# Products that read activations and write sums from the last column on, with weight halves at 64 and 128 bytes

## The reference

```python
z = jnp.einsum("bsd,de->bse", rmsnorm(x, g_mix), w_in)        # and w_qb, w_kvb
x = x + einsum(sigmoid(ga) * (oa @ w_oa) + sigmoid(gb) * (ob @ w_ob), w_o)
x = x + einsum(relu(einsum(rmsnorm(x), w_up)) ** 2, w_down)
x = x + sigmoid(einsum(rmsnorm(x), w_ple_gate)) * einsum(p, w_ple)
# second block, two layers: a gated delta rule (gdn_w_in, gdn_w_out), then forgetting
# attention (w_kv, fox_w_q, fox_w_o), each followed by
f = (silu(gu[..., :2816]) * gu[..., 2816:]) @ w_out            # gu = h @ w_in
x = x + rms_norm(f, post_ffn_norm)
```

## Time and profile before

| | |
|---|---|
| median of three runs | 2165.18 us |
| profiled execution | 2162.32 us |
| its span, first to last instruction | 2160.5 us |
| mean granted TensorE clock | 0.987 of 2.4 GHz |
| TensorE matmuls | 2095.5 us busy, 10710 instructions |
| TensorE weight loads | 1697.5 us busy, 10710 |
| VectorE, ScalarE, GpSimd | 1146.3, 816.6, 38.4 us busy |

### The profile page before, as it was taken

The page is one execution under the profiler, slowest core; times in us unless marked ns, Lnnn a source line. Parts: engine busy times, 40 slices in busy tenths (PEclk is TensorE's granted clock), DMA queues, the critical chain, the costliest instruction groups (busy, mean ns, idle before and its releaser), DMA issues. The chain is left out here.

```text
span 2160.5 us, 26090 instructions
## 1 busy us (share of the span) xinstructions
PE 2095.5 (97%) x10710; PEld 1697.5 (79%) x10710; DVE 1146.3 (53%) x1706; ACT 816.6 (38%) x1169; POOL 38.4 (2%) x34
## 2 busy tenths in 40 slices
PE   8999999999999999999999999999999899999998
PEld 6876678888888887787878888887786577888886
DVE  5674765542542579888846444324634736444423
ACT  4324753331232465542534222213325734322212
POOL 0120000000000000000100000000000000000000
PEclk9999999999999999999999999999999999999999
DMA  4220012223223222233122222222240031222221
GB/s 177 86 83 35 2 59 99 94 95 109 85 96 103 91 81 100 108 117 97 40 98 74 95 95 94 95 96 95 98 173 23 1 118 59 98 98 98 98 98 68
DMA packets 43111, 190.68 MB, mean 88 GB/s; under 512 B 15520, under 2 KB 16224, under 8 KB 22384
## 3 DMA queue, kind: packets, MB, share of 16 engines
q1 hardware_dynamic: 40656, 184.78, 25.0%
q10 hardware_dynamic: 2336, 4.23, 0.6%
HBM read 185.25 MB, written 3.74 MB: 87 GB/s over the span
## 5 line engine op out<-in xcount | busy, mean ns | idle before, releaser
L250 DVE TENSOR_TENSOR weights_low<-weights_raw,weights_high 128x2048 fp32r<-128x2048 f32 (+1 forms) x161 | 365.8, 2272 | 565.4 <-ACT weights_high L223 565.3
L441 PE MATMUL psum<-split,weights_high 128*128 128x512 f32 x1448 | 568.3, 392 | 8.3 <-PEq L146 4.2
L442 PE MATMUL psum<-split,weights_high 128*128 128x512 f32 x1448 | 564.6, 390 | 0.0
L443 PE MATMUL psum<-split,weights_low 128*128 128x512 f32 x1448 | 564.6, 390 | 0.0
L223 ACT CAST weights_high<-weights_raw 128x2048 fp32r<-128x2048 f32 (+1 forms) x161 | 304.0, 1888 | 545.3 <-PE psum L443 504.7
L441 PEld LDWEIGHTS psum<-split,weights_high 128*128 128x128 f32 x1448 | 272.2, 188 | 70.3 <-issue 8.4
L443 PEld LDWEIGHTS psum<-split,weights_low 128*128 128x128 f32 x1448 | 272.0, 188 | 57.4
L442 PEld LDWEIGHTS psum<-split,weights_high 128*128 128x128 f32 x1448 | 272.0, 188 | 56.0
L443 PE MATMUL psum<-hidden_high,weights_low 128*128 128x512 f32 x256 | 99.6, 389 | 0.0
L441 PE MATMUL psum<-hidden_high,weights_high 128*128 128x512 f32 x256 | 99.6, 389 | 0.0
L442 PE MATMUL psum<-hidden_low,weights_high 128*128 128x512 f32 x256 | 99.6, 389 | 0.0
(11 more groups left out here) (485 smaller groups left out, 3081.4 us busy)
## 6 DMA issues: line engine op xcount, KB each, us to landing
weights_raw<-in_weights SPq DMA_DIRECT2D x161, 1024.0 KB, 4.9
minus_c<-minus_c_rows ACTq DMA_DIRECT2D x16, 256.0 KB, 7.3
x_stream<-in_x SPq DMA_DIRECT2D x4, 512.0 KB, 7.1
gdn_in_grown<-gdn_rows SPq DMA_DIRECT2D x4, 512.0 KB, 4.7
chain_grown<-gdn_rows SPq DMA_DIRECT2D x4, 512.0 KB, 3.7
out<-end_results SPq DMA_DIRECT2D x8, 256.0 KB, 2.1
table<-rope_tables SPq DMA_DIRECT2D x1, 1024.0 KB, 12.0
weights_raw<-in_weights SPq DMA_DIRECT2D x1, 768.0 KB, 4.2
```

The costliest lines, as they stand in the source:

```text
L250: self.nc.vector.tensor_tensor(out=self.low_of(n)[:, 0:width], in0=self.raw[:, n % 2, 0:width], in1=self.high_of(n)[:, 0:width].bitcast(se ...
L441: nc.tensor.matmul(bank, wh, ah, start=first, stop=False)
L442: nc.tensor.matmul(bank, wh, al, start=False, stop=False)
L443: return nc.tensor.matmul(bank, wl, ah, start=False, stop=last)
```

## The change

All moving operands and all PSUM outputs of the two helpers get a step of -1: column 511 first, column 0 last. The order is the same on both sides, so each sum lands in its old place. The high and low halves of the weights become views of one tensor. Their slots start at 16 floats (even chunks) and 32 floats (odd chunks) past a multiple of 2048 floats, so 64 and 128 bytes past a multiple of 512 bytes; the filler grows from 40 to 136 floats, which together with the 32 floats at the tensor's end keeps the activations at a multiple of 512 bytes from `weights_raw`. The chunks kept apart stay in the arena.

```diff
+SLOT_OFFSETS = (16, 32)
-        self.high = enter(nc.sbuf_tensor("weights_high", [P, 2, CHUNK], f32r))
-        self.low = enter(nc.sbuf_tensor("weights_low", [P, 2, CHUNK], f32r))
+        halves = enter(nc.sbuf_tensor("weights_halves", [P, 4 * CHUNK + SLOT_OFFSETS[1]], f32r))
+        self.high, self.low = [[halves[:, at + n * CHUNK:at + (n + 1) * CHUNK] for n, at in zip((first, first + 2), SLOT_OFFSETS)]
+                               for first in range(2)]
...
-        return self.apart[n][0] if n in self.apart else self.high[:, n % 2, :]
+        return self.apart[n][0] if n in self.apart else self.high[n % 2]
...
-        enter(nc.sbuf_tensor("arena_offset", [P, 40], f32))
+        enter(nc.sbuf_tensor("arena_offset", [P, 136], f32))
...
+        def from_the_end(tile):
+            return tile[:, ::-1]
+
         def product(bank, w_parts, a_parts, first, last):
-            (wh, wl), (ah, al) = w_parts, a_parts
-            nc.tensor.matmul(bank, wh, ah, start=first, stop=False)
-            nc.tensor.matmul(bank, wh, al, start=False, stop=False)
-            return nc.tensor.matmul(bank, wl, ah, start=False, stop=last)
+            (wh, wl), (ah, al) = w_parts, (from_the_end(part) for part in a_parts)
+            out = from_the_end(bank)
+            nc.tensor.matmul(out, wh, ah, start=first, stop=False)
+            nc.tensor.matmul(out, wh, al, start=False, stop=False)
+            return nc.tensor.matmul(out, wl, ah, start=False, stop=last)
...
-            (wh, wl), (xh, xl) = w_parts, x_parts
-            columns = [(bank, slice(m * P, (m + 1) * P)) for m, bank in enumerate(banks)]
+            (wh, wl), (xh, xl) = w_parts, (from_the_end(part) for part in x_parts)
+            columns = [(from_the_end(psum[:, bank, :]), slice(m * P, (m + 1) * P)) for m, bank in enumerate(banks)]
```

More of the change, by code:

```diff
@@ L187, in high_of @@
     def high_of(self, n):
-        return self.apart[n][0] if n in self.apart else self.high[:, n % 2, :]
+        return self.apart[n][0] if n in self.apart else self.high[n % 2]
     def low_of(self, n):
-        return self.apart[n][1] if n in self.apart else self.low[:, n % 2, :]
+        return self.apart[n][1] if n in self.apart else self.low[n % 2]
     def load(self, sp, n):
@@ L239, in split_low @@
         pool.wait_ge(self.high_ready, chunk.number + 1)
-        self.nc.gpsimd.tensor_tensor(out=self.low[:, chunk.slot, 0:width],
+        self.nc.gpsimd.tensor_tensor(out=self.low[chunk.slot][:, 0:width],
                                      in0=self.raw[:, chunk.slot, 0:width],
-                                     in1=self.high[:, chunk.slot, 0:width].bitcast(self.f32),
+                                     in1=self.high[chunk.slot][:, 0:width].bitcast(self.f32),
                                      op=self.sub).then_inc(self.low_ready, 1)
@@ L435, in gain @@
             return gains[:, at:at + 1]
+        def from_the_end(tile):
+            return tile[:, ::-1]
         def product(bank, w_parts, a_parts, first, last):
-            (wh, wl), (ah, al) = w_parts, a_parts
-            nc.tensor.matmul(bank, wh, ah, start=first, stop=False)
-            nc.tensor.matmul(bank, wh, al, start=False, stop=False)
-            return nc.tensor.matmul(bank, wl, ah, start=False, stop=last)
+            (wh, wl), (ah, al) = w_parts, (from_the_end(part) for part in a_parts)
[3 more added lines that the diff above has]
+            return nc.tensor.matmul(out, wl, ah, start=False, stop=last)
         def product_by_parts(pe, k, banks, w_parts, x_parts, high_done, low_done):
-            (wh, wl), (xh, xl) = w_parts, x_parts
-            columns = [(bank, slice(m * P, (m + 1) * P)) for m, bank in enumerate(banks)]
+            (wh, wl), (xh, xl) = w_parts, (from_the_end(part) for part in x_parts)
+            columns = [(from_the_end(psum[:, bank, :]), slice(m * P, (m + 1) * P)) for m, bank in enumerate(banks)]
             pe.wait_ge(high_done, k + 1)
             for bank, sl in columns:
-                nc.tensor.matmul(psum[:, bank, :], wh[:, k, sl], xh, start=k == 0, stop=False)
-                nc.tensor.matmul(psum[:, bank, :], wl[:, k, sl], xh, start=False, stop=False)
+                nc.tensor.matmul(bank, wh[:, k, sl], xh, start=k == 0, stop=False)
+                nc.tensor.matmul(bank, wl[:, k, sl], xh, start=False, stop=False)
             pe.wait_ge(low_done, k + 1)
             for bank, sl in columns:
-                last = nc.tensor.matmul(psum[:, bank, :], wh[:, k, sl], xl, start=False, stop=k == DT - 1)
+                last = nc.tensor.matmul(bank, wh[:, k, sl], xl, start=False, stop=k == DT - 1)
                 if k == DT - 1:
```

## The result

The changed kernel takes 2209.98 us (median of four runs, 2205.84 to 2210.89), the one before 2165.14 us beside it: a ratio of 1.0205, with a 95% interval of [1.0187, 1.0222]. The forecast said 2122 and faster; the sign was wrong. The time lies just inside the upper end of the range, at the price of the rival "It never falls into step", but not for that rival's reason.

What follows compares the result with a forecast made beforehand. TensorE's product pace was taken as the bound. Backward order gave -48 us, offsets and splits nothing; less a tenth, -43 us from 2162.3 gave 2119, plus 2.9 to the median: 2122 us, with 8 in 10 between 2080 and 2210.

Steps and rivals of the forecast that it cites:

- It never falls into step: Rival, chance 0.30: every product stays at the unsettled 232.1 ns, 5.4 ns more each, +42 us, 2207 us.
- What bounds the kernel: TensorE's stream of 7788 products at 226.7 ns, 82% of the span; one ns of pace is worth 7.8 us.
- So the extra is no fixed price of a matmul: Product matmuls: the 32 clocks beyond 512 columns depend on how the next weights' load stands to the moving read.
- Step 1: All 7788 products, moving tiles and sums backward: pace falls to 220.5 ns, -6.2 ns each, -48 us.
- Step 2: Weight halves at 64 and 128 bytes: costs nothing by itself, judged from products at 192 and 256 bytes.
- The sign set for this step: Chunks kept apart at no offset, others at 64 or 128 bytes: differing paces would show step 2 wrong.
- Step 3: Splits into high and low halves: stay at 1.89 and 2.27 us, hidden by waits of 504.7 and 565.3 us.
- Nothing changes: Rival, chance 0.22: the steady 32 clocks come from the engine, not the addresses, and order does not matter; 2165 us.
- Backward access runs at half rate: Rival, chance 0.03: a step of -1 counts as non-contiguous and slows all products to half rate, +1577 us, 3742 us.

Runs made afterwards that it cites:

- c1: Changed kernel read forward without weight offsets, all but the first matmul of each sum cut to 384 columns: 1844.71 us.
- b3: Changed kernel, still backward, without weight offsets, all but the first matmul of each sum cut to 448 columns: 2043.96 us.
- b5: As b3, but with columns 2 to 449 in place of the first 448: 2044.06 us.
- m1: Changed kernel without weight offsets and forward, except that the third matmul of `product` reads and writes backward: 2175.84 us (2162.3 before).
- e1: Changed kernel with weight offsets set to 0, moving tiles and sums still backward: 2207.0 us, ratio 1.0204 against the kernel before.
- b1: Changed kernel, still backward, with weight halves at 256 (even chunks) and 384 bytes (odd): 2207.35 us.
- c2: Changed kernel, still backward, without weight offsets, all but the first matmul of each sum cut to 384 columns: 1874.86 us.
- e2: Changed kernel with moving tiles and sums forward again, weight halves still at 64 and 128 bytes: 2202.92 us, ratio 1.0184 against the kernel before.
- f3: Changed kernel read forward, weight halves at 256 (even chunks) and 384 bytes (odd): 2184.47 us.
- f2: Changed kernel read forward, weight halves at 192 (even chunks) and 320 bytes (odd): 2198.85 us.
- e4: Changed kernel with moving tiles read forward but sums still written backward, weight halves at 64 and 128 bytes (tokens mirrored): 2201.95 us.
- f4: Changed kernel read forward, weight halves at 224 (even chunks) and 240 bytes (odd): 2190.82 us.
- f5: Changed kernel read forward, weight halves at 8 (even chunks) and 248 bytes (odd): 2199.39 us.
- f1: Changed kernel read forward, weight halves at 16 (even chunks) and 32 bytes (odd): 2202.25 us.

## Why the prediction was wrong, point by point

- *What bounds the kernel.* Right: 7788 products, one ns of pace worth 7.8 us, nothing in TensorE's place. +6.67 ns gave 48.6 of 51.9 us.
- *"So the extra is no fixed price of a matmul: it depends on how the load of the next weights stands to the moving read."* Half right, and the half that failed carried the forecast. Forward, the place of the load beside the moving tile does move the step between 226.7 and 233.3 ns. But the steady 32 clocks are the same at 384 columns (c1), and the lowest at any place tried. The earlier trace rows showed ways of paying more than that, never less; I read them as proof that less could be had.
- *Step 1, "I take the middle between 225 and 216".* The step that failed. The lower end came from a plain-f32 matmul, another format, and the upper one from the shortest single duration of 1448, which is no pace; no row of these products showed a steady pace under 226.7. What the runs showed in its place is a price of the backward read itself: 48 clocks at 448 and 512 columns (b3, b5, m1), at 0 bytes as at the offsets (e1, b1) and with loads of 16, 80 and 128 columns, with the odd chunks at 236.7 ns and c2's 177.8 as the exceptions. The term is +6.67 ns instead of -6.2. It lies inside the bounds of 216 and 235 that I had set, but the gain was taken as the likelier side on rows that only showed losses.
- *Step 2, "Costed at nothing by itself".* Wrong forward: 39.6 us alone (e2). The earlier trace rows rest on 256 bytes, which has the step of 0 (f3). The earlier trace rows rest on the fast part of an 80-column product whose first steps were slow, and which was slow to its end at the same place in f3; a 128-column load at 192 bytes has 228.9 ns (f2). Neither row could show what 64 or 128 bytes do to a 128-column load. That the error didn't reach the sum was luck: the backward read costs its 233.3 ns at almost any offset. The sign set for this step shows little: the chunks kept apart have durations of 397 ns (median) like the rest, but some odd chunks have 236.7 ns. The Trainium skill's rule that the prediction weighed ("TensorE: Matmul & The Clock Gate", section What happens when you issue a matmul: independent read ports) would have made this nothing; e2's 1.0184 disagrees with it.
- *Step 3.* Right: 1.88 and 2.28 us, covered by waits of 535.8 and 591.2 us.
- *"Nothing changes".* It said that the 32 clocks come from the engine and not from the addresses. No run went below them, so far the runs agree; but order, which it held to change nothing, adds 16, and offsets add up to 16 forward.
- *"It never falls into step".* 2207 was nearly the right time for the wrong mechanism, by luck. Its price came from the 16-column product at 232.1 ns; that product itself now runs at a steady 233.3 ns. An uneven stream looks like e2's odd chunks, with single steps from 228 to 241 ns.
- *"Backward access runs at half rate".* Out. The rule cited there (the Trainium skill, "PSUM — Partial Sum Buffer", section Specifications: a non-contiguous access pattern slows matmuls) shows no effect for a step of -1: with the sums alone backward (e4) the time is 2201.95 us, against 2202.92 with them forward (e2).

Not tried: turning round the weights' own read. Open: why a backward read costs 16 clocks more, what sets the step at each place, and why one place can have two.

## What to carry to other kernels

Where fp32r matmuls of this shape follow each other without a gap, leave the moving operand in forward order and put stationary and moving tiles at the same place modulo 256 bytes; of ten places tried only that one had the shortest step nearly throughout, 240 bytes in most chunks and 16 bytes in a few. When a trace shows a steady price and some rows above it, the rows above bound a loss; they are no evidence for a gain below the steady one. And before an offset is called free, look at the same tile shape, at more than one offset, and at the whole product and not its steady end.

## What the runs showed of the hardware that was not expected

- An fp32r matmul's mean step is its columns plus 32 clocks forward (512: 226.7 ns, 384: 173.3) and plus 48 backward (512: 233.3, 448: 206.7; but 384: 177.8, plus 42.7), with weights and activations at the same place and a granted clock of 1.00 (2.4 GHz).
- The steady steps and the sums of these cycles are multiples of 16 clocks: 544, 560, two of 236 and 231 ns (1120), seven of e2's odd chunks (3904).
- Places near each other can differ by the whole price: 240 bytes 226.7 ns, 224 and 248 bytes 233.3 (f4, f5).
- One place can have two steady steps in one run: 226.7 and 233.3 ns at 16 bytes forward (f1, chunks 140 and 138), 233.3 and 236.7 ns at 128 bytes backward (the changed kernel, chunks 163 and 161).
- Moving columns 2 to 449 instead of 0 to 447 lengthened the weight load from 188 to 191 ns (medians of b3 and b5) and changed single steps from alternating 203 and 211 ns to a steady 207, with the same mean.
